# Eight gate modulation panels moved from the second layer's gate and output projections to the last layer's key and value projections

## The reference, cut to what matters

```python
mod = silu_c @ w_mod[l] + b_mod[l]                  # D x 3D
shift, scale, gate = jnp.split(mod[:, None, :], 3, axis=-1)
h = rmsnorm(x, norm_g[l]) * (1.0 + scale) + shift
...
x = x + gate * (y @ w_o[l])                         # layers 1 and 2
```

```python
shift_l, scale_l, gate_l = adaln_modulation(c, w_mod, b_mod)
h_lat = rms_norm(x_lat, norm_g) * (1 + scale_l[:, None]) + shift_l[:, None]
(na_q, na_k, na_v, ...) = jnp.split(h @ w_in, IN_SPLIT_POINTS, axis=-1)
y_na = neighbourhood_attention(lpart(q), lpart(k), lpart(v), cpart(k), cpart(v), na_rpb)
...
return x_lat + gate_l[:, None] * (merged @ w_out), None
```

## Time and profile before

| what | before |
|---|---|
| median of 3 runs | 4130.7 us (4128.36 to 4131.1) |
| the profiled execution, its own time | 4134.67 us |
| its span | 4132.9 us |
| TensorE busy, and mean granted clock | 3922.2 us (95%), 0.969 |
| VectorE, ScalarE, GpSimd busy | 1101.4, 654.0, 248.0 us |
| DMA | 489.69 MB, mean 118 GB/s |

### The profile page before, as it was taken

One profiled execution on the slowest core, in us unless ns is written; L12 is line 12 of the kernel. 1 busy time (PEld: TensorE's weight loads), 2 busy tenths in 40 slices (PEclk: granted clock), 3 DMA queues, 4 the chain that ended last, 5 costly groups with the idle time before them and its releaser, 6 DMA issues.

```text
span 4132.9 us, 60701 instructions
## 1 busy us (share of the span) xinstructions
PE 3922.2 (95%) x27010; PEld 2668.3 (65%) x27010; DVE 1101.4 (27%) x2366; ACT 654.0 (16%) x1509; POOL 248.0 (6%) x390
## 2 busy tenths in 40 slices
PE   5999999899999999969999999999999988999998
PEld 3446745554445666758748677666666667888887
DVE  1100143751002322212200531445554454000001
ACT  1100022420002122102100310222222222000000
POOL 0000000000000000240000000211111211000000
PEclk9999999999999999989999999999999986999999
DMA  8443323224333433496421134211111110544443
GB/s 337 176 153 122 123 92 112 82 84 180 144 132 122 156 130 123 163 183 255 163 82 64 59 123 133 66 40 44 44 44 34 34 33 5 168 152 153 152 157 122
DMA packets 77444, 489.69 MB, mean 118 GB/s; under 512 B 10480, under 2 KB 14576, under 8 KB 23552
## 3 DMA queue, kind: packets, MB, share of 16 engines
q1 hardware_dynamic: 70560, 462.45, 32.2%
q0 software_dynamic: 6624, 23.35, 2.3%
HBM read 481.57 MB, written 4.19 MB: 118 GB/s over the span
## 4 chain that ended last, share of the span: by engine, by line
PE 91%; DVE 3%; DMA 3%; ACT 1%; POOL 1%; issue 1%; DVEq 0%; ACTq 0%; POOLq 0%
PE ps L955 50%; PE ps L1055 9%; PE ps L949 7%; PE ps L1220 4%; PE ps L894 3%; PE ps L1015 3%; PE ps L1034 2%; PE ps L1205 2%; PE ps L952 2%; DMA w<-in_wi 2%; PE ps L1025 1%; POOL zone L832 1%; PE ps L902 1%; PE ps L1291 1%; PE ps L1124 1%
## 5 line engine op out<-in xcount | busy, mean ns | idle before, releaser
L955 PE MATMUL ps<-h,w 128*128 128x256 f32 (+1 forms) x4992 | 1554.9, 464 | 54.8 <-DMA w<-in_wi 37.3
L955 PEld LDWEIGHTS ps<-h,w 128*128 128x128 f32 x4992 | 943.5, 194 | 510.4 <-issue 412.7
L955 PE MATMUL ps<-y,w 128*128 128x256 f32 (+1 forms) x1792 | 507.9, 442 | 0.0
L955 PEld LDWEIGHTS ps<-y,w 128*128 128x128 f32 x1792 | 338.9, 190 | 153.9 <-issue 121.7
L1055 PE MATMUL ps<-h,w 128*128 128x256 f32 (+1 forms) x1024 | 413.2, 521 | 1.3 <-issue 1.3
L949 PE MATMUL ps<-w,h 128*128 128x256 f32 x1280 | 278.7, 380 | 0.0
L949 PEld LDWEIGHTS ps<-w,h 128*128 128x128 f32 x1280 | 243.6, 190 | 38.0 <-issue 6.1
L1055 PEld LDWEIGHTS ps<-h,w 128*128 128x128 f32 x1024 | 176.7, 194 | 91.4 <-issue 69.1
L1220 PEld LDWEIGHTS ps<-zone 64*64 64x64 f32 x4608 | 153.3, 139 | 47.6 <-issue 32.8
L832 POOL TENSOR_TENSOR zone<-zone 128x256 f32<-128x256 f32 x160 | 133.9, 851 | 796.1 <-ACT zone L1653 604.9
L894 PE MATMUL ps<-w,zone 128*32 128x256 f32 x2304 | 149.8, 403 | 29.6 <-DVE zone L2216 11.5
(11 more groups left out here) (306 smaller groups left out, 3109.0 us busy)
## 6 DMA issues: line engine op xcount, KB each, us to landing
w<-in_wm SPq DMA_DIRECT2D x144, 1024.0 KB, 8.0
w<-in_we SPq DMA_DIRECT2D x52, 1024.0 KB, 5.0
w<-in_w SPq DMA_DIRECT2D x48, 1024.0 KB, 5.1
w<-in_wmg SPq DMA_DIRECT2D x48, 1024.0 KB, 5.1
w<-in_wi SPq DMA_DIRECT2D x34, 1024.0 KB, 5.1
w<-in_wo SPq DMA_DIRECT2D x32, 1024.0 KB, 5.0
w<-in_wrw SPq DMA_DIRECT2D x32, 1024.0 KB, 5.1
w<-in_wbr SPq DMA_DIRECT2D x48, 512.0 KB, 4.4
```

The lines of the kernel that those rows point to most:

```text
L955: last = mm(pass_psum(s, q), rows[:, n * P:(n + 1) * P], src[k], start=(k == 0), stop=(k == s.kt - 1))
```

## The change

Only the first four gate panels and the first three output panels of the second layer are still followed by a modulation panel; the four key and four value panels of the last layer now are. The column mask gets a place of its own, so that GpSimd's wait goes. `gain2` is computed at output tile 7, behind the last scale panel. VectorE takes up the additions of the key and value projections before it adds the mask to the bias, and halves the gates after attention `n`, behind a wait for all 72 panels.

```diff
--- before.py
+++ after.py
@@ -449,7 +449,7 @@
         poolm = z(2048, 4, 2, NL)
         poolw = z(4096, 4, 2, NL)
         df = z(6144, 8, NL)
-        cmask = z(12288, 64)
+        cmask = z(13312, 64)
         merged = z(0, KT, NL)
         msig = z(4096, 3, 2, NL)
 
@@ -502,9 +502,12 @@
             lay(name, range(8))
         for name in ("d_kpe", "d_qp", "d_qn", "d_kn", "d_v"):
             lay(name)
-        lay("gate1", range(8))
-        lay("wo1", range(7))
-        for name in ("n_q", "n_k", "n_v", "p_u", "gate_n", "gate_p", "lo"):
+        lay("gate1", range(4))
+        lay("wo1", range(3))
+        lay("n_q")
+        for name in ("n_k", "n_v"):
+            lay(name, range(4))
+        for name in ("p_u", "gate_n", "gate_p", "lo"):
             lay(name)
         rw_first = len(ring)
         ring += [("rw", n) for n in range(16)]
@@ -804,7 +807,6 @@
                     pool.dma_start(rpb[half * GRID + c:half * GRID + c + 1, :, :, :].rearrange("p a b c -> p (a b) c"),
                                    A["rpb"][5 - half:11 - half, :, 63 - c:127 - c].rearrange("a b c -> (a b) c")
                                    .rearrange("(o a) c -> o a c", o=1)).then_inc(s_bias, 16)
-            pool.wait_ge(s_mrows, 72)
             pool.dma_start(cmask, A["c_col"]).then_inc(s_bias, 16)
             pool.wait_ge(s_x1, 1)
             pool.dma_start(spill, xl[:, :, :]).then_inc(s_spill, 16)
@@ -2319,10 +2321,11 @@
                 if n >= 1:
                     v_.tensor_tensor(lacc2, lacc2, lsq2[:, n % 2, :], ALU.add).then_inc(s_lacc, 1)
             run(value)
-            link(v_.tensor_tensor(gain2[:, :], gain[:, :, 0], ng[:, :, 3], ALU.mult))
             for t, _ in enumerate(residual("wo1", 1, (40, 14 + 7, T), [(xl, 0, 0)])):
                 if t == 0:
                     layer_mean(2, ps[:, 5, 0:NL], NL, lrc)
+                if t == 7:
+                    link(v_.tensor_tensor(gain2[:, :], gain[:, :, 0], ng[:, :, 3], ALU.mult))
                 if t == 1:
                     dve.wait_ge(s_lrt, 3)
                     link(v_.reciprocal(lrc, lrc))
@@ -2344,12 +2347,14 @@
             for t in range(KT):
                 last = v_.scalar_tensor_tensor(xl[:, t, :], xl[:, t, :], ng[:, t, 3:4], lr[:, 0:NL], ALU.mult, ALU.mult)
             last.then_inc(s_x1, 1)
-            link(v_.tensor_scalar(modc[:, 2, 2 * KT:, :], modc[:, 2, 2 * KT:, :], 0.5, None, ALU.mult))
-
+            run(adds("n_k"))
+            run(adds("n_v"))
             dve.wait_ge(s_bias, 16 * (2 + 2 * GRID))
             bv = rpb.rearrange("p a b c -> p (a b) c")
             link(v_.tensor_tensor(bv, bv, cmask.rearrange("p (o c) -> p o c", o=1).broadcast_to([P, 96, GRID]), ALU.add))
             attend("n", beside("n", adds))
+            dve.wait_ge(s_mod, 72)
+            link(v_.tensor_scalar(modc[:, 2, 2 * KT:, :], modc[:, 2, 2 * KT:, :], 0.5, None, ALU.mult))
 
             def pooled(n):
 
```

## The result

Over six executions each the changed kernel takes 4105.44 us (4103.25 to 4113.02) and the kernel before 4129.53 (4123.96 to 4141.66). The ratio is 0.9944, with a 95% interval of 0.9927 to 0.9960: faster by some 23 us, well clear of the noise. The forecast was 4107.

A forecast was written before the change was run, and what follows sets the result against it. TensorE was taken as the bound, standing still where weight halves come late. A net 22.9 us up to output panel 1 plus 0.5 before attention gave 23.4: 4111.3 in a profile, 4107 us for the median, range 4098 to 4116.

The forecast's parts named there:

- What bounds: Gate panels 4 to 7: 42.6 us of TensorE waits come from weight halves requested late and slowed by GpSimd's bias loads.
- The gate stretch: Gate panel 4 to output panel 1: output panel 1 starts 31.8 us earlier, less 8.9 for four later panels, net 22.9.
- the third, gate panel 7: Gate panel 7: halves take about 26 us, landing near 1804 and 1807; wait 4.1, clock 1.2, end about 1819.5.
- the bound below: Gate panel 7: halves follow the earlier ones directly and are there when wanted, at 1800 and 1803.5.
- the 23.4: Whole kernel: total gain in us, 22.9 net up to output panel 1 plus 0.5 before attention.
- The clock after a wait: Gate panels 5 to 7 and output panel 1: TensorE restarts on the low clock, costing about 1.2 us each time.
- the prompt loads: Rival, gate panels and output projection: halves wait only their turn beside bias packets; gain 31 us, 4100; chance 0.17.
- output panel 1: Output projection: its low half lands near 1839.5; wait 3 us, clock 1.2, start near 1840.5 instead of 1872.34.
- One modulation panel: Wherever it stands, TensorE pays 1.87 us for its rows and 0.36 for its columns, 2.23 in all.
- The new place: Key and value projections: eight panels at 2.23 us each come in; no DMA wait, taken as 0 (bounds 0 to 0.4).
- the mask addition: Last value panel's second pass, VectorE: done some 7 us before the first scores, cost 0; without that cover 6.56.
- The rival in which the new place becomes the bound: Value projection: low halves taking L us wait L - 5.3 plus 2.4 clock; gain gone at 8.9, 4141 at 9.5; chance 0.04.

The follow-up runs named there:

- (1): Kernel before, its 128 position bias loads issued only after the last query panel, modulation panels left alone: 4091.51 us, ratio 0.9898.
- experiment 9: Kernel before, position bias laid out on the host and loaded by one 3 MB load at the old place: 4093.16 us, ratio 0.9904.
- (4): Changed kernel, but all eight gate panels keep modulation panels, the output projection has none, seven go to key and value projections: 4138.87 us, ratio 1.0015.
- the second profile: Profile from timing the changed kernel again without edit, beside other runs on one chip: 4114.88 us, ratio 0.9945.
- Experiment 2: Changed kernel with the position bias loads issued only after the last query panel: 4117.99 us, ratio 0.9963.
- the paced kernel: Kernel before, GpSimd waiting before every fourth bias load until all earlier ones landed, so at most four stand in line: 4134.91 us, ratio 1.0002.

## Why the prediction was right, point by point

**What bounds.** That the waits are halves asked for late, each paying the latency under GpSimd's small loads, was argued and is now shown. Take the loads away (1) or make them one (9), and the waits go with every modulation panel in place. Free the output projection alone (4), and they stay. Nor is it a shortage of bandwidth: in experiment 9 GpSimd's 5 MB, in large pieces, were carried beside the same panels.

**The gate stretch.** Of the four waits predicted behind gate panel 4 (2.8, 2.2, 4.1, 3 us), the trace has 2.47, 2.55, none and 3.13, and a short one of 0.80. The step that failed is the third, gate panel 7: its halves were to take 26 us and land at 1804 and 1807, and they took 15.9 and 18.7 (16.1 and 19.4 in the second profile); in neither did gate panel 7 wait. I interpolated by the time of issue. Nearer to the truth was the bound below, that they follow close on the earlier halves: when they were asked for, SP's packets were already flowing (118 of them from 1774 to 1778, the last section shows more). The term was 4.1 + 1.2 = 5.3 us too large. It explains most of what the first profile has beyond the 23.4: 31.4 - 3.2 = 28.2.

**The clock after a wait** was priced at 1.2 us each time. In the first profile it came out anywhere from nothing to 1.7. After the wait of 2.47 us 48 matmuls took 10.63 us, as 48 without a wait did (10.61); after 3.13 us a pass took 8.83 for 7.15. The table of windows has the granted clock after the waits of 2.47 and 2.55 us, at full speed (2.4 GHz) after the one and at the 1.2 GHz level after the other:

```profile
1767.00:1769.00 2.00, 1.90 (x9) 1.69 (x10) 0.00 (x0) 0.00 (x0) 2.00 (x5) 1.00 1.02 49
1780.00:1782.00 2.00, 1.71 (x4) 1.47 (x5) 0.00 (x0) 0.00 (x0) 2.00 (x5) 0.50 1.03 248
```

**The number** is in part luck. From gate panel 4's first matmul to the first scores the kernel before takes 2274.88 - 1737.56 = 537.3 us, the first profile of the changed kernel 508.9 and the second 514.9. Gate panel 4, which the change leaves alone, took 0.7 more in the first and 3.9 less in the second. So the change itself gained 29.2 us in one execution and 18.5 in the other, on both sides of the 23.4. The first is nearer to the 31 of the prompt loads; in the second output panel 1 waited 6.83 us where 3 were predicted. The medians lie between.

**One modulation panel** was priced at 1.87 + 0.36 = 2.23 us. The real price is 2.5: a key panel with one takes 2062.79 - 2032.81 = 29.98 where it took 27.46 by SP's issues before. The rest lies in the panel's own two passes, which take 13.84 and 13.91 us to the next instruction, where half of 27.46 is 13.73. Four panels make 1.2 us less gain.

**The new place.** No wait in the key and value projections, as taken; the first scores start right behind panel 71's rows, and the mask addition was covered, by 9 us where I had said 7. The rival in which the new place becomes the bound was rightly priced in form, wait = latency - lead, with its point at a latency of 8.9. Experiment 2 made it happen by bringing the small loads there. It did so at the key panels, with a lead of 8.7 us, and the passes behind its two waits took 16.62 and 15.61 us for 14.00, so 2.6 and 1.6 of clock where 2.4 was priced. The halves' 5.1 us kept it away in the change itself.

**The nearest rivals.** Prompt loads (4100) would have been right for gate panel 7 and wrong for the halves before it (22.39 us for gate panel 6's). The Trainium skill's rule ("DMA: Bandwidth & Descriptors", Queues, rings and completion order) of queues served in turn, packet by packet, explains only a part of those: the trace agrees with it where SP's packets flow (363 of them beside 366 of GpSimd's), and not in the stretches before, where they stand still (last section). A half's latency fell to 7.8 us when the line of small loads was cut to four, so the length of GpSimd's line, or the rate of its packets, counts. How the engines come to make SP's packets wait for it, no run here shows.

## What to carry to other kernels

With a ring of few buffers, compare for each load its lead (from the release of its buffer to its use) with its latency at that place: the wait is the difference, here to 0.2 us wherever the chain names a low half behind a modulation panel, and a modulation panel in this two-buffer ring shortened the lead. Before moving the panels, look at who else is in the DMA queues. Here 3 MB in 256-byte pieces from another engine lengthened a half's latency from 5 to between 8 and 29 us, and moving those or making them one load gave twice the gain of the change.

## What had not been expected of the hardware

**The latency under the small loads is a standstill first, then an even turn.** The queues of the kernel before from 1762 to 1774, with four halves asked for by SP (1760.19 to 1771.85), and then from 1778 to 1790:

```profile
q0 software_dynamic: 678, 0.52, 99.5%
q1 hardware_dynamic: 9, 0.05, 6.3%
...
q1 hardware_dynamic: 363, 2.71, 89.3%
q0 software_dynamic: 366, 0.28, 11.8%
```

For twelve microseconds hardly a packet of SP's moves; then the two queues alternate, one packet for one, and SP, whose packets are larger, gets nine tenths of the bytes. The changed kernel's trace shows the same: 7 packets of SP's from 1758 to 1770, then 118 beside 119 from 1774 to 1778. A half asked for while SP's packets already flow, as gate panel 7's were, skips the standstill. The share of the engines misleads here. Worked out from these rows, one small packet takes 12 x 16 x 0.995 / 678 = 0.28 us in the standstill and 12 x 16 x 0.118 / 366 = 0.06 beside SP's, so by an estimate from these two the 546 packets of the earlier trace rows would fill a fifth of the engines at the second rate, where 91.9% is shown. What is waited for stays open.

**A short wait can cost nothing in clock, or most of its own length again.** In the paced kernel ten of the eleven passes behind waits of 2.2 to 3.3 us took 8.65 to 10.00 us against 7.15; the eleventh, after 2.41 us, took 7.14. That is 17.6 us for 29.6 of waits, while after the wait of 12.29 us the pass took 9.58, only 2.4 more. So the paced kernel's 33.9 us of waits come to 33.9 + 17.6 + 1.8 (gate panel 4) = 53 us, as much as the 42.6 + 8.3 = 51 of the kernel before, and the two times agree. Why one short wait of nearly the same length costs nothing and the next 1.7, no run here was made to tell.

**A shorter line.** With at most four small loads in line in place of some sixty, a projection half's latency fell from 18 to 26 us down to 7 to 8. The small loads themselves then landed in 7.3 us where they took about 30.
